# Layer 1's head rotations and the low half of its head results moved from GpSimd to VectorE, in a 1-core float32 network kernel on Trainium2

## The reference

```python
# keys, from layer 0's output (kvh = rmsnorm(x, kv_norm))
k1 = partial_rope(rmsnorm(k1, k_norm), cos, sin)       # k2 alike
# layer 1
q1 = partial_rope(rmsnorm(q1, b_q_norm[j]), cos, sin)  # q2 alike
o = diff_attention(q1, q2, k1, k2, v, lam)
o = rmsnorm(o, b_subln[j], SUBLN_EPS) * (1.0 - lam_init)
x = x + concat([o, memory_attention(...)]) @ w_o[l]

def partial_rope(x, cos, sin):   # rotates the first 16 of the 64 elements of each head
    x1, x2, xp = x[..., :8], x[..., 8:16], x[..., 16:]
    return concat([x1 * c - x2 * s, x1 * s + x2 * c, xp], axis=-1)
```

## Time and profile before

| | us |
|---|---|
| median of 3 runs | 1941.5 |
| lowest of them | 1940.02 |
| highest of them | 2093.22 |
| the profiled execution | 1944.71 |
| its span, first to last instruction | 1942.9 |

### The profile page before, as it was taken

The page is one execution under the profiler, slowest core; times in us unless marked ns, Lnnn a source line. Parts: engine busy times, 40 slices in busy tenths (PEclk is TensorE's granted clock), DMA queues, the critical chain, the costliest instruction groups (busy, mean ns, idle before and its releaser), DMA issues.

```text
span 1942.9 us, 21608 instructions
## 1 busy us (share of the span) xinstructions
PE 1835.7 (94%) x8477; PEld 1499.5 (77%) x8477; DVE 959.5 (49%) x1690; ACT 752.6 (39%) x1474; POOL 150.7 (8%) x181
## 2 busy tenths in 40 slices
PE   7899999999999998798999999998999889999997
PEld 5777888888887776577888888877777768888885
DVE  4556353434444655465444334379954454234345
ACT  6433252323234555464323323242765443222232
POOL 0011010101011111000101101010030000000000
PEclk9999999999999999799999999999999989999999
DMA  6222323233333211011333333322100223333331
GB/s 227 67 66 65 97 79 104 90 98 99 97 97 91 66 44 55 22 44 42 102 95 99 97 98 98 98 72 86 49 12 1 76 89 103 96 95 96 97 98 54
DMA packets 195748, 158.37 MB, mean 82 GB/s; under 512 B 5248, under 2 KB 161152, under 8 KB 195648
## 3 DMA queue, kind: packets, MB, share of 16 engines
q1 hardware_dynamic: 194240, 154.16, 25.9%
q0 software_dynamic: 400, 1.25, 0.3%
q10 hardware_dynamic: 1008, 1.59, 0.2%
HBM read 154.88 MB, written 2.10 MB: 81 GB/s over the span
## 4 chain that ended last, share of the span: by engine, by line
PE 83%; DVE 12%; ACT 3%; issue 1%; DMA 0%; ACTq 0%; DVEq 0%
PE ps L758 27%; PE ps L760 26%; PE ps L759 26%; DVE sb L2255 3%; DVE sb L1860 2%; PE ps L810 1%; PE ps L1189 1%; DVE sb L2381 1%; DVE sb L1874 0%; DVE sb L1858 0%; DVE sb L2020 0%; PE ps L1077 0%; PE ps L1083 0%; DMA sb<-in_con 0%; ACT sb L1408 0%
## 5 line engine op out<-in xcount | busy, mean ns | idle before, releaser
L758 PE MATMUL ps<-sb,sb 128*128 128x512 f32 (+4 forms) x2547 | 998.8, 395 | 32.5 <-DVE sb L2110 8.4
L759 PE MATMUL ps<-sb,sb 128*128 128x512 f32 (+4 forms) x2547 | 975.0, 384 | 0.0
L760 PE MATMUL ps<-sb,sb 128*128 128x512 f32 (+4 forms) x2547 | 974.2, 384 | 0.0
L758 PEld LDWEIGHTS ps<-sb,sb 128*128 128x128 f32 (+1 forms) x2547 | 484.2, 191 | 144.8 <-issue 19.0
L760 PEld LDWEIGHTS ps<-sb,sb 128*128 128x128 f32 (+1 forms) x2547 | 484.3, 191 | 94.1
L759 PEld LDWEIGHTS ps<-sb,sb 128*128 128x128 f32 (+1 forms) x2547 | 485.3, 192 | 87.4
L1860 DVE TENSOR_TENSOR sb<-sb,sb 128x512 fp32r<-128x512 f32 x532 | 357.8, 714 | 353.7 <-ACT sb L1387 352.7
L1387 ACT ACTIVATE sb<-sb 128x512 fp32r<-128x512 f32 x532 | 304.4, 622 | 445.2 <-PE ps L760 445.1
L2059 DVE TENSOR_TENSOR sb<-sb,sb 128x512 fp32r<-128x512 f32 x64 | 68.1, 1063 | 177.0 <-ACT sb L1529 176.8
L1539 ACT ACTIVATE sb<-ps 128x512 f32<-128x512 f32 x64 | 38.3, 598 | 208.3 <-PE ps L760 208.3
L656 POOL TENSOR_TENSOR sb<-sb 128x512 f32<-128x512 f32 x64 | 66.8, 1044 | 608.1 <-ACT sb L1539 608.1
(11 more groups left out here) (202 smaller groups left out, 1048.2 us busy)
## 6 DMA issues: line engine op xcount, KB each, us to landing
sb<-in_w_up SPq DMA_DIRECT2D x86, 512.0 KB, 3.9
sb<-in_w_down SPq DMA_DIRECT2D x86, 512.0 KB, 3.9
sb<-in_w_gate SPq DMA_DIRECT2D x22, 512.0 KB, 3.7
sb<-in_a_w_in SPq DMA_DIRECT2D x20, 512.0 KB, 3.7
sb<-in_w_in SPq DMA_DIRECT2D x20, 512.0 KB, 3.6
sb<-in_w_o SPq DMA_DIRECT2D x16, 512.0 KB, 3.9
sb<-in_w_mem_kv SPq DMA_DIRECT2D x8, 512.0 KB, 7.3
sb<-in_w_out SPq DMA_DIRECT2D x8, 512.0 KB, 3.9
```

Of the source, the lines that this page charges most:

```text
L758: mm(ps, lh, rh, start=start, stop=False, **k)
L759: mm(ps, lh, rl, start=False, stop=False, **k)
L760: return mm(ps, ll, rh, start=False, stop=stop, **k)
```

## The change

VectorE rotates: queries right behind `rsqrt_a` in `na`, keys right behind the multiply in `nb`, with the same four instructions and the same waits between them. VectorE also writes the low half in `C`. GpSimd's loop over the plan is gone. The tables, the tiles and the order of all other work stay.

```diff
@@ gpsimd_program @@
                 TTT(TC[w][:, :, j, :], con[:, :, 0, :], g, ALU.mult).then_inc(S("rope_t"), 1)
                 TTT(TS[w][:, :, j, :], con[:, :, 1, :], g, ALU.mult).then_inc(S("rope_t"), 1)
-        q.wait_ge(S("rope_t"), 8)
-
-        def rope(buf, t):
...
-            if w == "Q":
-                q.wait_ge(S("head_sq"), B.head[buf, t] + 1)
-            else:
-                q.wait_ge(S("head"), B.key[buf, t] + 1)
-            q.wait_ge(S("roped"), 2 * n)
-            TTT(tr, x, s, ALU.mult).then_inc(S("rope"), 1)
...
-        for slot in B.plan:
-            for s in slot:
-                if s[0] in ("na", "nb") and s[1:] in B.rope and (s[0] == "na") == (s[1][0] == "Q"):
-                    rope(*s[1:])
-                elif s[0] == "C":
-                    g = s[1]
-                    hi, lo = CC[HEADS[g]]
-                    q.wait_ge(S("sub_hi"), g + 1)
-                    TTT(lo[:, :], OT[:, :], hi[:, :].bitcast(F32), ALU.subtract).then_inc(S("sub_lo"), 1)
         mlp(1)
@@ vector_program @@
+        def rope(buf, t):
+            n, w = B.rope[buf, t], buf[0]
+            heads = 4 if buf in ("QB", "KB") else 8
+            v = ROWS[buf][:, t, 0:64 * heads].rearrange("p (h d) -> p h d", h=heads)
+            x1, x2 = v[:, :, 0:8], v[:, :, 8:16]
+            x = v[:, :, 0:16]
+            tr = TR[:, 0:heads, :]
+            c = TC[w][:, t, :, :].rearrange("p j d -> p (j d)").unsqueeze(1).broadcast_to([128, heads, 16])
+            s = TS[w][:, t, :, :].rearrange("p j d -> p (j d)").unsqueeze(1).broadcast_to([128, heads, 16])
+            q.wait_ge(S("rope_t"), 8)
+            if w == "K":
+                q.wait_ge(S("head"), B.key[buf, t] + 1)
+            q.wait_ge(S("roped"), 2 * n)
+            tt(tr, x, s, ALU.mult).then_inc(S("rope"), 1)
+            q.wait_ge(S("rope"), 2 * n + 1)
+            tt(x, x, c, ALU.mult).then_inc(S("rope"), 1)
+            q.wait_ge(S("rope"), 2 * n + 2)
+            tt(x1, x1, tr[:, :, 8:16], ALU.subtract).then_inc(S("roped"), 1)
+            tt(x2, x2, tr[:, :, 0:8], ALU.add).then_inc(S("roped"), 1)
+
         def unit_step(kind, *a):
             step = (kind,) + a
             if kind in ("rt", "T"):
@@ na @@
                 rsqrt_a(("B",) + a, st, n, m, eps)
+                if buf[0] == "Q":
+                    rope(buf, t)
             elif kind == "nb":
@@ after N @@
                 stt(OT[:, :], banks[B.tb][:, :], SUBG, OS[:, :], ALU.mult, ALU.mult).then_inc(S("sub_d"), 1)
+            elif kind == "C":
+                g = a[0]
+                hi, lo = CC[HEADS[g]]
+                q.wait_ge(S("sub_hi"), g + 1)
+                tt(lo[:, :], OT[:, :], hi[:, :].bitcast(F32), ALU.subtract).then_inc(S("sub_lo"), 1)
```

## The result

The changed kernel takes 1952.5 us (median of 22 runs), the kernel before 1940.8 us in the same comparison (22 runs). The ratio is 1.0058, 95% interval 1.0043 to 1.0073: 11.3 us slower, with 8.3 to 14.2 us as the interval. That is less than 2%, but the interval excludes no change. The forecast was 1952.6. Three launches lay far above all others (2093 and 7227 us before, 3672 us after); they are in the medians, and the ratio leaves them out.

The account below looks back on a forecast made before the run. TensorE, busy 94%, was taken as the bound, with VectorE's work costing time only where TensorE waits for it. QB 2.0, KB 2.6, QA 1.7, KA 2.8, `C` 0 and clock 2.0 sum to +11.1 us: 1952.6, range 1945 to 1961.

Parts of the forecast that it names:

- QB, +2.0: At QB's norms, three rotations of 0.68 us on VectorE stand ahead of the low half TensorE needs: +2.0 us.
- KB, +2.6: At KB's norms, three key rotations less 0.54 us idle, plus a fourth ahead of line 1920: +2.6 us.
- QA, +1.7: At QA's norms, three rotations on the path add 2.6 us and contention gives back 0.9: +1.7 us.
- KA, +2.8: At KA's norms, four rotations add 4.0 us, contention returns 1.2; TensorE's wait goes from 5.5 to 8.3 us: +2.8.
- The price of a rotation: On VectorE, 0.68 us with 4 heads and 0.88 with 8; key rotations 0.79 and 0.99 us.
- The clock, +2.0 for all four: TensorE's granted clock around the four norms: longer waits may lower it, costing +2.0 us together, with ends -2 and +10.
- VectorE's busy time, +17: Sign over the whole kernel: VectorE busy about 17 us longer, 13.4 for rotations plus 6 x 0.7, less contention.
- The rule against the sum: VectorE and GpSimd share an SBUF read port; if this held for every instruction, the change would be faster.
- Hidden: Rival: rotations at QB, KB and QA vanish in VectorE's idle time, only KA pays +2.8, so 1944.3 us; chance 0.15.
- Contention decides: Rival: at QA, KA and `C`, removed GpSimd contention outweighs the rotations; 1937.2 us with rotations at nothing; chance 0.06.
- VectorE stalls in `C`: Rival: each low half in `C`, waiting for ScalarE's copy, delays the next maxima; 4 us more, 1956.6; chance 0.07.
- The clock falls at QB and KB for long: Rival: two slow TensorE stretches of 3.4 us, 1957.4 us, or 1960.8 if QA's and KA's grow too; chance 0.2.

Follow-up runs that it names:

- e7: Changed kernel with the first multiply of each VectorE rotation made four times instead of once; ratio to the kernel before 1.0086.
- e8: Changed kernel with GpSimd also doing all its old rotation instructions, on tiles of its own that nobody reads; ratio to the kernel before 1.0068.
- e1: Kernel before with only the low halves of `C` moved to VectorE, GpSimd still rotating; ratio to the kernel before 0.9999, -0.2 us.
- e9: Changed kernel, but VectorE rotates only QB and KB and GpSimd rotates QA and KA; ratio to the kernel before 1.0053, +10.3 us.
- e10: Changed kernel, but VectorE rotates only QA and KA and GpSimd rotates QB and KB; ratio to the kernel before 1.0010, +1.9 us.
- e2: Kernel before with only the rotations moved to VectorE, GpSimd still writing the low halves of `C`; ratio to the kernel before 1.0071, +13.8 us.
- e3: Changed kernel with KA's transposes two slots later in the plan; ratio to the kernel before 1.0054, +10.5 us.
- e6: Changed kernel with QA's and KA's transposes four slots later in the plan; 1944.1 us, ratio to the kernel before 1.0012.
- e11: Changed kernel with each rotation's first multiply made four times, measured again with more rounds; ratio to the kernel before 1.0105.
- e5: Kernel before with QA's and KA's transposes four slots later in the plan, GpSimd rotating; 1931.9 us, ratio to the kernel before 0.9947.

## Why the prediction was right

*The whole.* By the count above the waits grew by 9.0 us, where the four terms for the norms make 9.1. The stage from QB's first norm to the MLP, 627.6 to 907.9 us, grew by some 10 us, inside the 5 to 17 that the prediction allowed.

*QB, +2.0.* Measured 1.9 in the changed kernel, and e7's +2.3 for 3 x 0.77 us. The first rotation did vanish in idle time (1.41 became 0.69 us).

*KB, +2.6.* Measured 2.7.

*QA, +1.7.* TensorE's waits there grew by 1.6 us. Of its two parts, the rotations and the 0.9 us of contention given back, e8 shows the second by itself: 1.0 us.

*KA, +2.8.* The wait grew by 2.8 us, to 8.3 as stated. The two parts were each a little small: a rotation takes 1.04 us, not 0.99, and e8 puts the contention at 1.4 us, not 1.2.

*C, 0.* e1: -0.2 us, interval -3.1 to +2.5, with no wait changed.

*The price of a rotation.* 0.22 us for 64 elements, 0.19 for 32, 0.29 for 128, each within 0.02 us of what the two nearest shapes gave. Operands broadcast over the heads and runs of 8 and 16 elements cost nothing extra that shows.

*The clock, +2.0 for all four.* The sum held, its parts did not, so here the hit is in part luck. In the profiled execution the clock is about +5.9 us between KB and QA and -4.8 behind KA, and over the whole stage +0.9. The medians of e9 and e10 put it at +5.8 us with QB and KB (10.3 less 4.5) and -2.6 with QA and KA (1.9 less 4.5), each within some 4 us either way; their own profiled executions have +3.9 and +2.0. Its sign at QA and KA stays open. This is the term that was mis-sized in its parts: behind KB a slow stretch like QA's 6.8 us, at a cost of 3.4 us at most, was foreseen; e2, e3, e6, e8 and e9 had that, and the changed kernel's execution had 13.7 us. That slow time between KA and the MLP changes from one execution to the next was not in the prediction at all, and it happened to offset the other.

*VectorE's busy time, +17.* It grew by 11.2 us, so this sign was missed. The rotations add 11.6 us of busy time, not 13.4, for that sum counts the steps of 0.03 us between instructions, in which VectorE isn't busy; `C` adds 3.5, not 4.2. The other 3.9 us are contention that went, 2.3 of them where nobody waited: line 1860, now 1828, fell from 800 to 685 ns over 20 instructions.

*The rivals.* "Hidden" falls by the waits at QB, KB and QA. "Contention decides" falls by its size: e8 puts it at 3.1 us. "VectorE stalls in `C`" falls by e1. "The clock falls at QB and KB for long" came half true, at KB and not at QB; with the longer rotations of e7 and e11 it fell at QB too, at 634 us.

*The rule against the sum.* That a VectorE instruction with two SBUF inputs and a GpSimd one that reads SBUF hold each other up (the Trainium skill, "SBUF — State Buffer", section "Who interferes with whom") is borne out by e8, on both engines, and the VectorE instruction at 715.52, which ended just behind GpSimd's, fits a hold to the end. What the rule doesn't give is the price, for not all that GpSimd does meets an instruction of VectorE for which somebody waits; TensorE's waits put it at 3.1 us.

## What to carry to other kernels

What an instruction costs is read from who waits behind it, not from how busy its engine is: VectorE was half idle, and still 14 of 16 rotations went onto the path, at full length but for 0.54 us of idle time at KB, since they stood ahead of the one low half that TensorE waited for. The same reading points to the repair. TensorE had independent pieces to do, and moving its transposes four slots later won 10 us, while moving the rotations to VectorE, all or half of them, won nothing. GpSimd was the better place for this short work, its contention (3.1 us in e8) included.

A change of a few us is read from waits and granted clock together. A total that comes out right can hide two errors in the clock that cancel, as here.

## What was not expected of the hardware

The clock makes single profiles uncertain by several microseconds, as much as many changes are worth. From KA's restart to the MLP TensorE has the same instructions and waits in nine kernels, and they took 139.8 us in e1, 140.0 in the changed kernel and in e7, 140.4 in e11, 142.4 in e8, 144.8 before and in e10, 145.3 in e9 and 145.6 in e2.

At KB the granted clock fell to its lower level of 1.2 GHz in all eight kernels in which VectorE rotates KB. In six of them TensorE had waited 1.1 to 1.5 us and then 2.5 us there, with full-speed matmuls between, and in e7 and e11 3.4 us at once. Where it had waited only 1.1 us at KB, the clock fell in two kernels of five. At QA it fell in eleven kernels, with 2.4 us of waiting or more, and in neither of the two whose later transposes had taken most of that waiting away (0.3 us left in e5, at most 0.8 us at once in e6).
